# Hybrid diffusion step: the normalised input stays in SBUF over the convolution, and 24 of 96 gate pieces run between the transforms

## What is computed

```python
proj = n @ P['w_in'][l]
hy, q_a, kv_a, k_r, fn, gates = jnp.split(proj, [i0, i1, i2, i3, i4], axis=-1)
u = short_conv(u, conv_w, conv_b)
x1, x2, v = jnp.split(u, 3, axis=-1)
z = x1 * fftconv(v, filt_f[:, 0], skip[0])
z = x2 * fftconv(z, filt_f[:, 1], skip[1])
y_b = blocked_attention(q, k, v) @ P['w_mla_o'][l]          # 8 heads
f = jnp.fft.fft2(f, axes=(1, 3), norm='ortho').real
g_a, g_b, g_c = jnp.split(jax.nn.sigmoid(gates), N_BRANCH, axis=-1)
y = (g_a * y_a + g_b * y_b + g_c * y_c) @ P['w_out'][l]
```

## Time and profile before

| | us |
|---|---|
| median of 3 runs | 3219.79 (3218.14 to 3223.1) |
| profiled execution | 3221.59 |
| its span | 3219.8 |
| PE busy | 3103.7 (96% of the span) |
| DVE busy | 1742.7 (54%) |
| ACT busy | 966.3 (30%) |

### The profile page before, as it was taken

The page is one execution under the profiler, slowest core; times in us unless marked ns, Lnnn a source line. Parts: engine busy times, 40 slices in busy tenths (PEclk is TensorE's granted clock), DMA queues, the critical chain, the costliest instruction groups (busy, mean ns, idle before and its releaser), DMA issues.

```text
span 3219.8 us, 47826 instructions
## 1 busy us (share of the span) xinstructions
PE 3103.7 (96%) x20540; PEld 3028.7 (94%) x20540; DVE 1742.7 (54%) x2873; ACT 966.3 (30%) x1445; POOL 47.4 (1%) x92
## 2 busy tenths in 40 slices
PE   7999999988999999999999999999899999999998
PEld 4999999987999899999999999998789989999998
DVE  7656666646555655343465565655655545643334
ACT  3422322313444432121232121232244443322222
POOL 0000000000000000000000000000000000000000
PEclk9999999999999999999999999999999999999999
DMA  8255542455122523232223333345522252322221
GB/s 306 85 197 195 230 158 105 190 221 200 70 73 107 196 87 125 92 118 80 104 80 137 131 149 127 141 162 224 232 77 74 88 198 95 118 84 75 79 76 63
DMA packets 78933, 430.61 MB, mean 134 GB/s; under 512 B 8849, under 2 KB 12369, under 8 KB 46722
## 3 DMA queue, kind: packets, MB, share of 16 engines
q1 hardware_dynamic: 58656, 324.56, 27.3%
q0 software_dynamic: 9504, 56.78, 4.6%
q10 hardware_dynamic: 10562, 46.21, 3.6%
HBM read 370.73 MB, written 56.79 MB: 133 GB/s over the span
## 4 chain that ended last, share of the span: by engine, by line
PE 78%; DVE 11%; ACT 4%; issue 3%; DMA 3%; DVEq 0%; ACTq 0%
PE tile_psum L566 38%; PE tile_psum L573 19%; PE tile_psum L918 4%; PE tile_psum L527 3%; PE tile_psum L492 3%; PE tile_psum L922 2%; PE misc_psum L492 2%; PE tile_psum L774 2%; PE tile_psum L532 2%; DVE wlo L1614 1%; ACT whi L1159 1%; DMA raw<-in_w_mix 1%; DVE h L1770 1%; PE tile_psum L971 1%; DVE n_lo L1692 1%
## 5 line engine op out<-in xcount | busy, mean ns | idle before, releaser
L566 PE MATMUL tile_psum<-n_hi,whi 128*128 128x320 f32 x3264 | 746.5, 309 | 4.0 <-issue 2.2
L566 PE MATMUL tile_psum<-n_lo,whi 128*128 128x320 f32 x3264 | 744.3, 309 | 0.0
L566 PEld LDWEIGHTS tile_psum<-n_hi,whi 128*128 128x128 f32 x3264 | 546.8, 188 | 6.8 <-DVE n_lo L1692 4.2
L1614 DVE TENSOR_TENSOR wlo<-raw,whi 128x2048 fp32r<-128x2048 f32 (+2 forms) x202 | 443.5, 2195 | 193.0 <-ACT whi L1159 190.7
L566 PEld LDWEIGHTS tile_psum<-n_lo,whi 128*128 128x128 f32 x3264 | 547.5, 188 | 0.0
L573 PE MATMUL tile_psum<-n_hi,wlo 128*128 128x320 f32 x3264 | 512.3, 308 | 0.0
L573 PEld LDWEIGHTS tile_psum<-n_hi,wlo 128*128 128x128 f32 x3264 | 486.9, 188 | 0.0
L1159 ACT ACTIVATE whi<-raw 128x2048 fp32r<-128x2048 f32 (+2 forms) x202 | 369.8, 1831 | 369.4 <-DMA raw<-in_w_up 178.8
L566 PE MATMUL tile_psum<-x_hi,whi 128*128 128x320 f32 x1408 | 321.3, 309 | 0.0
L566 PE MATMUL tile_psum<-x_lo,whi 128*128 128x320 f32 x1408 | 320.6, 308 | 0.0
L1826 DVE TENSOR_TENSOR hidden<-gate_act,tile_psum 128x320 f32<-128x320 f32 x176 | 85.6, 486 | 375.6 <-ACT gate_act L1258 375.2
(11 more groups left out here) (285 smaller groups left out, 3606.6 us busy)
## 6 DMA issues: line engine op xcount, KB each, us to landing
raw<-in_w_up SPq DMA_DIRECT2D x88, 1024.0 KB, 4.8
w_ada<-in_w_ada SPq DMA_DIRECT2D x128, 512.0 KB, 5.7
raw<-in_w_down SPq DMA_DIRECT2D x32, 1024.0 KB, 4.8
raw<-in_w_gate SPq DMA_DIRECT2D x24, 1024.0 KB, 4.8
whi<-table_keep SPq DMA_DIRECT2D x20, 1024.0 KB, 4.7
wlo<-table_keep SPq DMA_DIRECT2D x20, 1024.0 KB, 7.4
g_keep<-gate_out POOLq DMA_DIRECT2D x48, 320.0 KB, 2.4
gates<-g_keep POOLq DMA_DIRECT2D x16, 960.0 KB, 6.0
```

Of the source, the lines that this page charges most:

```text
L566: pe.matmul(tps[:, t.s, m, 0:TH], blk(p, m * n + k)[0], (hi, lo)[b][:, k, tok], start=k == 0 and b == 0, stop=False)
L1614: dve.tensor_tensor(wlo[:, r, 0:cols], raw[:, r, 0:cols], whi[:, r, 0:cols].bitcast(F32), ALU.subtract)\
```

## The change

1. `n_hi`, `n_lo` are no longer stored and loaded back. `fnet_mid_hi` and `fnet_mid_lo` move to the place of `x_hi` and `x_lo`, and one filter buffer `fq` serves both convolutions; the second filter is loaded after the last forward tile of the first.
2. The steps stand in a new order (`HYENA_ORDER`): `channels`, `low_sums` and the token products first, then the two convolutions, with 24 gate pieces between their parts. `low_spread` and `queries` move behind the second convolution's forward tiles.
3. The panels are loaded in the order `RING`. `head_order()` starts with piece 24 and leaves out the pieces behind the first and the fifth S of each head, those behind P, two at Q0 and Q1, and the last ones.
4. `inverse` writes one half of its output to the `head_tile` slot and the other to a `misc` slot.

```diff
-TABLE_ORDER = (0, 1, 2, 3, 4, 5, 0, 1, 2, 3)
+RING = [("kept", 4), ("kept", 5), ("kept", 0), ("kept", 1), ("gate", 0), ("kept", 2), ("kept", 3), ("gate", 1), ("kept", 0), ("kept", 1),
+        ("gate", 2), ("kept", 2), ("kept", 3)]
+HEADS_AT = len(RING)
+RING += [("heads", 0), ("gate", 3), ("gate", 4), ("gate", 5), ("heads", 1), ("gate", 6), ("gate", 7), ("heads", 2), ("gate", 8), ("gate", 9),
+         ("heads", 3), ("gate", 10), ("gate", 11)]
...
-                    order += [("Q", hd), ("F", 0)] + [("F", 0)] * (n == 0) + [("K", hd)] * (hd % 2 == 0) + [("QS", hd)] + [("F", 0)] * (hd == 0)
-            order += [("S", n), ("F", 0)]
+                    order += [("Q", hd), ("F", 0)] + [("K", hd)] * (hd % 2 == 0) + [("QS", hd)] + [("F", 0)] * (hd == 0)
+            order += [("S", n)] + [("F", 0)] * (n % 5 not in (0, 4))
...
-                order += [("P", (n - 2) // 5)] + [("F", 0)] * (n not in (6, 11, 16, 21))
+                order += [("P", (n - 2) // 5)]
...
-    order += [("F", 0)] * 2
...
-    for panel in range(2, 18):
+    for panel in range(HEADS_AT + 2, len(RING) + 2):
...
-TURNS = [("turn", 0), ("channels", 0), ("channels", 1), ("forward", 0, 0), ("channels", 2), ("forward", 0, 1)]
-TURNS += [("forward", 0, 2), ("channels", 3), ("forward", 0, 3), ("forward", 0, 4), ("channels", 4), ("low_sums",)]
-CONVOLVE = [("inverse", 0), ("low_spread",), ("tokens", 0), ("turn", 1), ("tokens", 1), ("forward", 1, 0), ("tokens", 2)]
-CONVOLVE += [("forward", 1, 1), ("queries",)] + [("forward", 1, f) for f in range(2, 5)] + [("inverse", 1)]
+HYENA_ORDER = [("channels", t) for t in range(5)] + [("low_sums",), ("tokens", 0), ("turn", 0), ("tokens", 1), ("tokens", 2)]
+HYENA_ORDER += [("forward", 0, 0), ("forward", 0, 1), ("R", GATE_POS[0]), ("forward", 0, 2), ("L", GATE_POS[0]), ("forward", 0, 3), ("forward", 0, 4)]
+HYENA_ORDER += [("F", f) for f in range(8)] + [("R", GATE_POS[1]), ("L", GATE_POS[1]), ("inverse", 0)] + [("F", f) for f in range(8, 16)]
+HYENA_ORDER += [("turn", 1), ("forward", 1, 0), ("forward", 1, 1), ("R", GATE_POS[2]), ("forward", 1, 2), ("L", GATE_POS[2])]
+HYENA_ORDER += [("forward", 1, 3), ("forward", 1, 4)] + [("F", f) for f in range(16, 20)] + [("low_spread",)] + [("F", f) for f in range(20, 24)]
+HYENA_ORDER += [("queries",), ("inverse", 1)]
...
-        (fah, fal), _ = place(N0, ("fnet_mid_hi", [P, 5, 512], F32R), ("fnet_mid_lo", [P, 5, 512], F32R))
+        (fah,), _ = place(X0 + 2 * XT, ("fnet_mid_hi", [P, 5, 512], F32R))
+        (fal,), _ = place(XL + 2 * XT, ("fnet_mid_lo", [P, 5, 512], F32R))
...
+        (fq,), _ = place(base + 4 * 10 * HYW, ("filter_freq", [P, 5, 2 * HYW], F32))
...
+                    take = ((tps, slots.head_tile), (mps, slots.misc))
...
-                act.dma_start(n_keep[0], nh[:, :, :].bitcast(F32)).then_inc(n_spilled, 16)
-                act.dma_start(n_keep[1], nl[:, :, :].bitcast(F32)).then_inc(n_spilled, 16)
...
+                    if (o, f) == (0, 4):
+                        act.dma_start(fq[:, :, :], fq_keep[l, 1].rearrange("f p c -> p f c")).then_inc(fq_in[1], 16)
...
+                def after_fill(f):
+
+                    if f >= 2 and f % 2 == 0:
+                        gate_job(f // 2 - 1)
```

More of the change, by code:

```diff
@@ L388, in program @@
         sg_out, hid_hi, hid_ready = sem("gate_act_out"), sem("hidden_hi"), sem("hidden_ready")
-        n_spilled, h_spilled = sem("n_spilled"), sem("h_spilled")
-        back = [sem(f"n_back{half}") for half in range(2)]
+        h_spilled = sem("h_spilled")
         table_kept = [sem(f"table_kept{i}") for i in range(6)]
@@ L891, in low_spread @@
                         ins.then_inc(misc_done[m], 1)
-                steps = {"turn": turn, "low_sums": low_sums, "forward": forward, "channels": channels, "low_spread": low_spread,
-                         "inverse": inverse, "tokens": tokens, "queries": queries}
-                for what, *which in MIX_ORDER:
-                    steps[what](*which)
-                pe.wait_ge(low_split, due(low_split, 4))
-                all_read(tile_free)
-                back_at = [due(back[0], 32), due(back[1], 16)]
-                panel0, job0 = at[0], 48 * l
-                at[0] += 16
-                keys, vals, turned = [None] * HEADS, None, None
                 def part_of_gate(f):
-                    q, p = f // 2, panel0 + f // 24 * 4 + 1 + f // 8 % 3
+                    q, p = f // 2, panel0 + GATE_POS[f // 8]
                     out, b0, tok = tps[:, 1, q % 2, 0:TH], q // 2 % 2 * KT, slice(q % 2 * TH, (q % 2 + 1) * TH)
+                    if f == 0:
+                        all_read(tile_free)
                     if f % 2 == 0:
@@ L924, in part_of_gate, with elsewhere @@
                         freed[p] = (fill_done, job0 + q + 1)
+                def elsewhere(n):
+                    pass
+                steps = {"turn": turn, "low_sums": low_sums, "forward": forward, "channels": channels, "low_spread": low_spread,
+                         "inverse": inverse, "tokens": tokens, "queries": queries, "F": part_of_gate, "R": elsewhere, "L": elsewhere}
+                for what, *which in HYENA_ORDER:
+                    steps[what](*which)
+                pe.wait_ge(low_split, due(low_split, 4))
+                keys, vals, turned = [None] * HEADS, None, None
                 for what, n in HEAD_ORDER:
                     h_, qt = n // 5, n % 5
-                    s = panel0 + n // 2 * 4
                     if what == "Q":
+                        s = panel0 + HEAD_POS[n // 2]
                         if n % 2 == 0:
@@ L1506, in inverse, with gate_job, elsewhere @@
                     rotary_keys(kh)
[L1507 to L1510 removed]
+                    round_at(HEADS_AT)
+                    round_at(HEADS_AT + 1)
+                def gate_job(q):
+                    act.wait_ge(fill_done, 48 * l + q + 1)
+                    if l or q >= 4:
+                        act.wait_ge(g_kept[q // 2 % 2], 16 * (12 * l + q // 4))
+                    act.activation(gate_out[q // 2 % 2][:, q % 2 * TH:(q % 2 + 1) * TH], tps[:, 1, q % 2, 0:TH], ACT.Copy).then_inc(fill_free, 1)
+                def after_fill(f):
+                    if f >= 2 and f % 2 == 0:
+                        gate_job(f // 2 - 1)
+                def elsewhere(n):
+                    pass
                 steps = {"turn": turn, "low_sums": low_sums, "forward": forward, "channels": channels, "low_spread": low_spread,
[L1513 to L1514 removed]
+                         "inverse": inverse, "tokens": tokens, "queries": queries, "F": after_fill, "R": round_at, "L": elsewhere}
+                for what, *which in HYENA_ORDER:
                     steps[what](*which)
@@ L2168, in _ @@
                 rotary_keys(kh, kl)
-                split_panel()
+                split_at(HEADS_AT + 1)
                 def keep_z():
```

137 lines of the change are left out of this document (67 added, 70 removed).

## The result

The changed kernel takes 3281.27 us (median of 4 runs, 3273.45 to 3290.79), the kernel before 3220.47 in the same series: 1.019 times as long, 95% interval 1.0161 to 1.0219, or 61 us more. The profiled execution took 3278.81 with a span of 3277.0.

The account below looks back on a forecast made before the run. PE's own matmuls were taken to bound the kernel (78% of the chain). Convolutions 2 x 31.9, heads -12.2 and -14.6, clock +2.6 sum to +39.6 us on 3219.79: forecast 3259, 80% range 3228 to 3276.

Parts of the forecast that it names:

- the term for the clock: Time lost to PE's slower clock: 1.3 us per layer in the heads, 1.5 us in each convolution.
- V0: Place in the heads where PE would wait 5.8 us for the first exponential.
- rival 4: More goes wrong in the convolution, stalls remaining beside the pieces: at most +42 us a layer, kernel 3280; chance 10%.
- Convolution: Stage forecast at 131.2 us, +31.9 per layer: work 115.8, waits 13.9, clock 1.5.
- F18: Piece among the second forwards; PE waits 4.9 us for ACT's copy of half tile 7, behind five roundings.
- F4: Piece behind the first forwards; PE waits 1.7 us for ACT's copy of half tile 0.
- rival 3: The copies aren't late, so F4 and F18 wait for nothing: 2 x 6.6 us less, kernel 3246; chance 12%.
- Heads: Stage forecast at 286.2 us before the clock: 12.2 less in the first layer, 14.6 less in the second.
- Q2 to Q4: Stretch of the heads forecast at 74.3 us, 4.9 longer than before with four pieces fewer.
- T13: Place in the heads where PE waits 3.65 us because roundings R19 and R20 stand ahead of T12's on ACT.
- The spill: Storing the normalised input, costed at nothing, hidden behind the mix projections; its removal gives at most 2.8 us.
- Rival 1: The heads' waits don't grow, every removed piece returns its 1.76 us: -10.4 us a layer, kernel 3199; chance 9%.

Follow-up runs that it names:

- Run 1: Changed kernel with 24 extra, unused pieces per layer in the heads, at the places the change had emptied; ratio 1.0226 to the kernel before, median 3294.44 us.
- run 4: Changed kernel with the copies of half gate tiles 0 and 7 moved earlier on ACT alone; ratio 1.0126 to the kernel before, median 3262.56 us.
- run 5: As run 4, with the second turn also placed between pieces 11 and 12 instead of behind piece 15; ratio 1.011 to the kernel before, median 3257.32 us.
- run 7: Changed kernel with 16 extra, unused pieces per layer, only behind the first and fifth score tile of each head; ratio 1.0196 to the kernel before, 3284.57 us.
- run 8: Changed kernel with 8 pieces in the convolution instead of 24, roundings 7, 5 or, last version, 10 places later; ratios 0.9998, 0.9993, 0.9975 to the kernel before.
- run 3: As run 2, but PE's wait for all tile slots moved ahead of Q0, as in the kernel before; ratio 0.9999 to the kernel before, 3221.28 us.
- run 9: As run 3, with rounding and split of panels 7 places behind the slot's last use instead of 5; ratio 1.0004 to the kernel before, 3222.65 us.
- run 2: Changed kernel with all 96 gate pieces back in the heads and none between the transforms; ratio 1.0032 to the kernel before, median 3232.72 us.
- run 6: As run 5, with rounding and split of panels 10 places behind the slot's last use instead of 5; ratio 1.0016 to the kernel before, 3227.09 us.

## Why the prediction was wrong

The direction, the places and the waits that grow were right. The time was forecast at 3259 and measured at 3281.27, above the range's end of 3276.

**The step that failed is the term for the clock**: "With more stalls this must happen more often; 1.3 us per layer" for the heads, and 1.5 for the convolution. Measured, the slower clock takes 15.3 and 15.2 us of the two layers' heads (0.94 of 254.22 and 253.35) and 4.9 and 7.6 of the two convolutions (0.96 of 123.64, 0.94 of 125.94). I had the row that could have sized it, 0.89 in the only stretch of the heads that began behind a long stall, or 14.23 x 0.11 = 1.6 us for one stall, and had counted some 45 us of waits into those heads; I then priced the clock as if that stretch stayed the only one. Run 1 shows that the clock came from the waits: the same lists with the gaps filled ran at 0.99.

The whole term is 43.0 us where 5.6 were forecast, a difference of 37.4, and the span was missed by only 17.6. That the total came no further off was luck: other terms were too high and hid part of it. The clearest case is V0. It was to wait 5.8 us and was idle for 2.85, but the stretch ahead of it ran at 0.86, which lengthened its matmuls by 2.4; the slow clock stood inside the forecast wait. And 3281 is nearly the 3280 of rival 4, but not by its mechanism: it put +42.3 on each convolution, where +35.9 and +38.0 were measured, and left the heads as forecast.

Point by point:

- *Convolution, 131.2 forecast, 135.16 and 137.25 measured.* Idle 11.5 and 11.3 against 13.9; the clock 4.9 and 7.6 against 1.5; busy time at full clock 118.7 against the 115.8 counted from start to start. The wait at F18 was 4.35 against 4.9, that at F4 0.8 against 1.7, that behind the turn 2.3 against 2.3. Runs 4 and 5 took away what the forecast had named, and the time with it. I had priced rival 3 (the copies aren't late) at 13 us; run 4 gained 19, because the clock came along.
- *Heads, 287.5 with the clock forecast, 294.49 and 295.19 measured.* The stretches came to 23.8, 16.4, 29.2, 75.5, 74.6 and 75.0 against 23.6, 15.4, 27.0, 74.3, 70.2 and 75.7. Q2 to Q4 did get longer with fewer pieces. The wait of T13 behind R19 and R20 was 3.88 against 3.65, and the one of Q4 3.9 against 3.7, the one of T9 2.87 against 3.55. Idle time was 40.3 where the text expected some 45 (its new waits, counted from start to start, add up to 51.8), so the waits were counted high, which hid part of the error in the clock.
- *The spill, forecast at nothing.* It was worth 4.9 us up to the end of the first layer's mix stage, 3.1 of them the wait above: two large stores stood beside the loads of the mix panels. I had looked only for PE's waits in the convolution, not in the stage in which the stores ran.
- *Sum.* Against +39.6 the span grew by 57.2: heads 7.0 and 7.7 too low, convolution 4.0 and 6.0 too low, the rest of the program 7.1 too high.
- *Rival 1 (the heads' waits don't grow)* needed them to grow by less than 10.4 us; they grew by 24.5. The rule of the Trainium skill that stood beside it, "Perfetto Trace Analysis", section "Optimization Strategy" (interleave regimes with different most-contended engines), is not borne out by a run here. Eight pieces moved gave 0.9998 and 0.9993 with 7 and 5 places, 24 moved gave 1.019, and only with roundings 10 places later did the kernel gain 7.5 us. In the heads PE's pieces were themselves the other half of such an interleaving, and taking 24 of them out raised the idle time there from 15.8 to 40.3 us.

What stays open: which of the 24 places is nearly free (run 7), and what part of the gain of run 8's last version the eight moved pieces have. That `ROUND_LAG = 10` is right for 88 pieces where 5 and 7 are alike was measured, not explained.

## What to carry to other kernels

Work that covers a latency chain is worth far less when it is taken away than its own duration: of 42.3 us moved out of the heads, 4 to 6 came back. Before moving filler, ask of each place what PE will wait for there afterwards, and move only as many pieces as the new place has idle time for; here even eight, placed so, gained nothing by themselves. Where waits grow, price the slower clock for each long wait, by a stretch that already has one. The share of that stretch taken for the whole stage would have been too much here: 0.11 of 254 is 28 us, and 15.3 were measured. And when filler becomes sparse, weight roundings and splits that were harmless between it stand in the chain: their places must be chosen anew.

## What was not expected of the hardware

The slower clock follows the idle time, though not by it alone. In the first layer's heads, some 280 to 306 us long and with the same kinds of work, the granted clock was 0.99 or 0.98 at 15.8 to 18.7 us idle (before, runs 1, 3, 9), 0.98 or 0.97 at 19.9 to 21.7 (runs 2 and 8), 0.96 at 23.6 (run 7), 0.95 at 27.8 (run 6) and 0.94 at 38.4 to 40.3 (runs 4, 5, changed). The same 19.9 us went with 0.97 once and with 0.98 once. And two stores of 2560 KB went with a slowing of the loads of 1024 KB beside them, from 4.8 us to 14.3 from issue to landing, although stores and loads were in different queues (issued by ACT and by SP).
